# The low part of the forget-sum rows, made by VectorE one step earlier, and the rows' memset moved ahead of it

## The chip, the cores and the metric

The kernel runs on one core of a Trainium2 chip. The metric is the device time in microseconds of one launch. The engines that matter here are TensorE (PE in the profile, its weight loads PEld), VectorE (DVE), ScalarE (ACT) and SyncE (SP), which issues the loads of the weights. Every engine works through its own instructions in order, and they are tied by semaphores.

## The reference, cut to what matters

The program is one DeltaNet block followed by two hybrid layers (L = 0 and 1) on 256 positions of width 1024. The change is in the forgetting attention of the hybrid layers, with 8 heads of 128 channels:

```
log_f = log_sigmoid(ff + b_f)                 # (256 positions, 8 heads)
cum   = cumsum(log_f, axis=positions)
s     = q . k / sqrt(128) + (cum[query] - cum[key])
s     = where(key <= query, s, -inf)
p     = softmax(s);  o = p . v
```

The term `cum[key]` is the same for all queries of a head, so it is a row over the 256 keys. The kernel adds it to the scores by one matmul. That matmul rounds its operands, so each row is held as two parts, a rounded high part and a low part that is the rest; the two are added up by the contraction.

## The kernel before

**The stream.** All large weights come as a stream of chunks of 128 x 2048 values (1 MB each), 93 chunks in each hybrid layer. Chunk n goes through four steps. SyncE loads it into one of four slots of `raw` as soon as the chunk four before it is done. ScalarE's `prep(n)` rounds it to the high weights `w_hi`, in one of two slots, when TensorE is done with chunk n-2. VectorE's `prep(n)` (line 1612) subtracts that from `raw` and so makes the low weights `w_lo`. TensorE then does 48 matmuls in each of two halves, high by high, low by high and high by low (lines 351 to 353, called by `mm3`). ScalarE last copies the result out of PSUM (line 1082 in these stages).

**The order.** It is written out by hand for each engine. In the loop `group(off, after)`, step c of VectorE and ScalarE prepares chunk off+c+2 first, and then runs what the list `after[c]` holds. TensorE does chunk off+c and then its own `after[c]`. So at step c, VectorE's extra work sits behind low weights that can be made only when TensorE has finished chunk off+c, since these need the high weights, and the high weights need the slot of that chunk.

**The forget sums.** VectorE's `ff_log` makes the negated log forget gates and spreads them into `nlf_rep`. TensorE's `cum`, behind its second chunk of the group `L_FV` (c = 1), sums them into PSUM bank 7: columns 16 to 31 for the queries, and columns 256 to 511 of partitions 0 to 63 for the keys' rows. VectorE's `cum` (line 2140) copies the first of these, ScalarE's `row_hi` (line 1439) waits for that copy and then writes the high part of the rows into `fox_rows`, and VectorE's `row_lo` subtracts it from PSUM (line 2149) and copies a last piece (line 2150). The tile `fox_rows` has 128 partitions; those from 64 on are set to zero once, by a memset in `row_lo` of L = 0 (line 2147).

**The scores.** TensorE waits for those rows behind its third chunk (c = 2) and makes the scores of heads 0 to 3; the fourth chunk follows, and then heads 4 to 7:

```
def fox_scores(h0):
    if h0 == 0:
        pe.wait_ge(S("evicted"), j0 + L_FV)
        pe.wait_ge(S("row_ready"), L + 1)
...
        mm(ps[:, bank, 0:P + T], sel_r[:, h:h + 1].to_broadcast([P, P]), fox_rows[:, :], start=True, stop=False, skip_group_check=True)
        mm(ps[:, bank, 0:P], q[:, 0:P], k[:, 0:P], start=False, stop=True, skip_group_check=True)
        mm(ps[:, bank, P:P + T], q[:, P:T], k, start=False, stop=True, skip_group_check=True)\
...
group(tok_chunk, L_FV, 1, [None, cum, lambda: fox_scores(0), lambda: fox_scores(4)])
```

These three matmuls have the lines 933 to 935. VectorE's `fox_scores` takes each head out of PSUM by two instructions (lines 2156 and 2157); for heads 4 to 7 TensorE waits until the head four before has been taken out, as they share a bank. ScalarE's list for the same group is `[None, row_hi]`. In what follows, the chunks of the group `L_FV` are called first, second, third and fourth, and the one behind them is the first of the group `L_RQK`.

Of the kernel before, what the change touches and what calls it, by code (L numbers as in the profile page):

```python
# [16 lines left out]
P = 128  # L17
# [73 lines left out]
def build_program(nc, io, layers=LAYERS):  # L91
    f32, f32r = mybir.dt.float32, mybir.dt.float32r
# [5 lines left out]
    with ctx:  # L98
# [9 lines left out]
        def at(name, shape, offset, dt=f32):  # L108
            return nc.alloc_sbuf_tensor_at(name, shape, dt, offset=offset)
# [21 lines left out]
        fox_rows = at("fox_rows", [P, 3 * P], place[0] + 4 * N_CB, f32r)  # L131
# [29 lines left out]
        def S(name):  # L161
            if name not in sems:
                sems[name] = ctx.enter_context(nc.semaphore(name))
            return sems[name]
# [24 lines left out]
        def bmid(ap, n):  # L189

            ap = ap.unsqueeze(1)
            return ap.to_broadcast([ap.shape[0], n, ap.shape[2]])
# [1410 lines left out]
        def _(dve):  # L1603
            order = Order(dve, "dve_order")
# [3 lines left out]
            def prep(n, s4, s2):  # L1608
                if isinstance(n, int) and n >= total:
                    return  # L1610
                dve.wait_ge(S("hi_ready"), n + 1)
                tt(w_lo[:, s2, :], raw[:, s4, :], w_hi[:, s2, :].bitcast(f32), ALU.subtract).then_inc(S("lo_ready"), 1)  # L1612
# [91 lines left out]
            def softplus(dst, z, e, m, n):  # L1704

                t1, t2 = sm[:, 11, 0:n], z
                order(ts(t1, e, 2.0, None, ALU.add))
                order(nc.vector.reciprocal(t1, t1))
                order(tt(t2, e, t1, ALU.mult))
                order(tt(t1, t2, t2, ALU.mult))  # L1710
                order(ts(e, t1, 1.0 / 17, 1.0 / 15, ALU.mult, ALU.add))
                for odd in (13, 11, 9, 7, 5, 3, 1):
                    order(tt(e, e, t1, ALU.mult))
                    order(ts(e, e, 1.0 / odd, None, ALU.add))
                order(tt(e, e, t2, ALU.mult))
                order(stt(dst, e, 2.0, m, ALU.mult, ALU.add))
# [375 lines left out]
            for L in range(layers):  # L2092
# [17 lines left out]
                def group(off, after=(), n0=n0):  # L2110

                    for c in range(4):
                        n = n0 + off + c
                        prep(n + 2, (n + 2) % RAW, n % 2)
                        for f in (after[c] if c < len(after) else ()):
                            f()
# [12 lines left out]
                def ff_log():  # L2129
                    dve.wait_ge(S("ff_exp"), L + 1)  # L2130
                    softplus(sm[:, 0, 0:16], sm[:, 2, 0:16], sm[:, 3, 0:16], sm[:, 0, 0:16], 16)

                    order(ts(sm[:, 1, 0:16], sm[:, 0, 0:16], math.sqrt(P), None, ALU.mult))
                    for t in range(2):
                        ins = nc.vector.tensor_copy(nlf_rep[:, t, :].rearrange("p (r h) -> p r h", h=8), bmid(sm[:, 1, t * 8:t * 8 + 8], 8))
                    ins.then_inc(S("nlf_ready"), 1)
# [6 lines left out]

                def row_lo():
                    dve.wait_ge(S("row_hi"), L + 1)
                    if L == 0:
                        order.mark(nc.vector.memset(fox_rows[64:P, :].bitcast(f32), 0.0))
                    rows_hi = fox_rows[32:64, P:3 * P]
                    order(tt(rows_hi, ps[32:64, 7, T:2 * T], rows_hi.bitcast(f32), ALU.subtract))
                    nc.vector.tensor_copy(fox_rows[0:64, 0:P], fox_rows[0:64, P:2 * P].bitcast(f32)).then_inc(S("row_ready"), 1)  # L2150

                def fox_scores(h0):
                    for h in range(h0, h0 + 4):
                        bank = 4 + h % 4
                        dve.wait_ge(S("fox_s_mm"), L * 8 + h + 1)
                        order.mark(stt(fox_s[:, h, 0:P], ps[:, bank, 0:P], sm[:, 5, h:h + 1], fm[:, P:T], ALU.add, ALU.add))
                        stt(fox_s[:, h, P:3 * P], ps[:, bank, P:3 * P], sm[:, 5, 8 + h:9 + h], fm, ALU.add, ALU.add)\
                            .then_inc(S("fox_s_ev"), 1)
# [154 lines left out]

                job(n0 + L_FQK, 4)
                group(L_FQK + 4, [[lam], [], [ff], [ff_log]])
                group(L_FV, [[], [cum], [row_lo, lambda: fox_scores(0)], [lambda: fox_scores(4)]])
                group(L_RQK, [[fox_max], [], [], [fox_norm]])
                group(L_RV)
                group(L_LX, [[lo_of(sp_ + 1, s4, 0)], [rope_sin], [rope_cos], [rope_add]])
# [190 lines left out]
```

## Time and profile before

| what | value |
|---|---|
| time, median of 3 runs | 1783.1 us (1782.43 to 1783.38) |
| profiled execution, its own time | 1776.84 us |
| its span, first to last instruction | 1775.0 us |
| TensorE matmuls busy | 1681.6 us, 95% of the span |
| VectorE busy | 1099.2 us, 62% |
| ScalarE busy | 813.8 us, 46% |
| mean granted TensorE clock | 0.988 |
| moved by DMA | 331.40 MB, mean 187 GB/s |

The profiled execution is one execution, and its time lies 1.84 us above its span. Busy times are unions over overlapping instructions. A busy TensorE may still be a slowly clocked one, so the granted clock stands beside it.

### The profile page before, as it was taken

The numbers are of one execution on the slowest core, as the hardware profiler recorded it, in microseconds if no ns is written. First come the engines' busy times: TensorE is split into PE (matmuls) and PEld (weight loads), VectorE is DVE, ScalarE is ACT, GpSimd is POOL, SyncE is SP. The second block draws the span as 40 slices with busy tenths as digits, with TensorE's granted clock in tenths as the row PEclk, the third lists the DMA queues.
The fourth block names the chain that finished last, engine by engine and source line by source line (L and its number), as shares of the span: only waits on it lengthen the run. The fifth ranks groups of instructions, "written<-read, shape, count | busy, mean of one in ns | idle before, by whom it ended". The sixth has DMA issues, their size and how long they took to land.

```text
span 1775.0 us, 34458 instructions
## 1 busy us (share of the span) xinstructions
PE 1681.6 (95%) x15290; PEld 1585.4 (89%) x15290; DVE 1099.2 (62%) x1379; ACT 813.8 (46%) x1053; POOL 34.3 (2%) x68
## 2 busy tenths in 40 slices
PE   5998899999999989999999999989899999999997
PEld 4896788799988889999999899979899999979997
DVE  4476754589853555568775755565547778666463
ACT  3335424433333535447655444435354575445352
POOL 0000000000000000000000000000000000000000
PEclk8999999999999999999999999999999999999999
DMA  9776533564558445545455355535354445535551
GB/s 393 281 286 235 195 145 129 207 214 165 211 211 324 177 155 157 175 146 188 167 190 188 114 190 197 179 107 190 122 188 167 167 167 191 190 111 194 194 190 71
DMA packets 45529, 331.40 MB, mean 187 GB/s; under 512 B 5072, under 2 KB 5072, under 8 KB 5456
## 3 DMA queue, kind: packets, MB, share of 16 engines
q1 hardware_dynamic: 36032, 260.73, 42.7%
q0 software_dynamic: 9216, 67.11, 10.0%
q8 instruction: 113, 1.85, 0.4%
q10 hardware_dynamic: 144, 1.51, 0.2%
q14 instruction: 24, 0.20, 0.0%
HBM read 326.18 MB, written 1.05 MB: 184 GB/s over the span
## 4 chain that ended last, share of the span: by engine, by line
PE 76%; DVE 11%; ACT 7%; DMA 3%; issue 1%; SPq 0%; POOL 0%; ACTq 0%; DVEq 0%; POOLq 0%
PE ps L351 20%; PE ps L352 19%; PE ps L353 19%; DVE w_lo L1612 4%; PE ps L404 4%; ACT w_hi L1071 4%; PE ps L476 3%; PE ps L455 2%; DMA ada_raw<-ada 2%; DMA ada<-ada 1%; PE ps L639 1%; PE ps L650 1%; DVE rstd L1659 1%; DVE rsq L2353 1%; DVE x L1697 1%
## 5 line engine op out<-in xcount | busy, mean ns | idle before, releaser
L1612 DVE TENSOR_TENSOR w_lo<-raw,w_hi 128x2048 fp32r<-128x2048 f32 x207 | 474.4, 2292 | 477.0 <-ACT w_hi L1071 476.6
L351 PE MATMUL ps<-act_hi,w_hi 128*128 128x256 f32 x2672 | 755.2, 283 | 14.2 <-DVE act_lo L1681 4.6
L352 PE MATMUL ps<-act_lo,w_hi 128*128 128x256 f32 x2672 | 743.8, 278 | 0.0
L353 PE MATMUL ps<-act_hi,w_lo 128*128 128x256 f32 x2672 | 743.7, 278 | 0.0
L1071 ACT ACTIVATE w_hi<-raw 128x2048 fp32r<-128x2048 f32 (+1 forms) x229 | 421.9, 1842 | 544.4 <-PE ps L353 527.2
L351 PEld LDWEIGHTS ps<-act_hi,w_hi 128*128 128x128 f32 x2672 | 504.9, 189 | 24.7 <-issue 16.3
L352 PEld LDWEIGHTS ps<-act_lo,w_hi 128*128 128x128 f32 x2672 | 503.5, 188 | 1.1 <-issue 0.2
L353 PEld LDWEIGHTS ps<-act_hi,w_lo 128*128 128x128 f32 x2672 | 503.3, 188 | 0.0
L351 PE MATMUL ps<-mlp_hi,w_hi 128*128 128x256 f32 x512 | 143.3, 280 | 0.4
L352 PE MATMUL ps<-mlp_lo,w_hi 128*128 128x256 f32 x512 | 141.8, 277 | 0.0
L353 PE MATMUL ps<-mlp_hi,w_lo 128*128 128x256 f32 x512 | 141.7, 277 | 0.0
L351 PEld LDWEIGHTS ps<-mlp_hi,w_hi 128*128 128x128 f32 x512 | 96.3, 188 | 1.1 <-DVE w_lo L1620 1.0
L2037 DVE SCALAR_TENSOR_TENSOR gacc<-gpad,vectors,gacc 128x256 f32<-128x256 f32 x176 | 84.5, 481 | 19.7 <-ACT gacc L1344 14.3
L352 PEld LDWEIGHTS ps<-mlp_lo,w_hi 128*128 128x128 f32 x512 | 96.2, 188 | 0.2
L353 PEld LDWEIGHTS ps<-mlp_hi,w_lo 128*128 128x128 f32 x512 | 96.2, 188 | 0.0
L404 PE MATMUL ps<-h_up,raw 128*128 128x256 f32 x352 | 82.4, 386 | 2.0 <-ACT h_up L1334 1.6
L404 PEld LDWEIGHTS ps<-h_up,raw 128*128 128x128 f32 x352 | 65.4, 192 | 13.5 <-ACT h_up L1334 3.0
L351 PE MATMUL ps<-w_hi,act_hi 128*128 128x256 f32 x256 | 72.4, 283 | 0.0
L353 PE MATMUL ps<-w_hi,act_lo 128*128 128x256 f32 x256 | 71.3, 279 | 0.0
L352 PE MATMUL ps<-w_lo,act_hi 128*128 128x256 f32 x256 | 71.3, 278 | 0.0
L476 PE MATMUL ps<-ada_raw,silu_c_wide 128*32 128x256 f32 x1024 | 64.1, 389 | 6.4 <-DMA ada_raw<-ada 6.4
L476 PEld LDWEIGHTS ps<-ada_raw,silu_c_wide 128*32 128x32 f32 x1024 | 30.1, 111 | 30.3 <-DMA ada_raw<-ada 9.0
(414 smaller groups left out, 2015.8 us busy)
## 6 DMA issues: line engine op xcount, KB each, us to landing
raw<-stream SPq DMA_DIRECT2D x233, 1024.0 KB, 4.9
ada_raw<-ada POOLq DMA_DIRECT2D x64, 1024.0 KB, 7.1
ada_f<-ada SPq DMA_DIRECT2D x4, 1024.0 KB, 13.9
ada_a<-ada SPq DMA_DIRECT2D x3, 1024.0 KB, 19.6
s<-s SPq DMA_DIRECT2D x4, 512.0 KB, 10.0
consts_stage<-consts_a SPq DMA_DIRECT2D x1, 1728.0 KB, 32.8
consts_stage<-consts_b ACTq DMA_DIRECT2D x1, 1472.0 KB, 9.8
x<-xT SPq DMA_DIRECT2D x1, 1024.0 KB, 7.0
```

The costliest lines, as they stand in the source:

```text
L351: mm(out, ah, bh, start=first, stop=False, skip_group_check=shared)
L352: mm(out, ah, bl, start=False, stop=False, skip_group_check=shared)
L353: return mm(out, al, bh, start=False, stop=last, skip_group_check=shared)
L404: mm(ps[:, bank, 0:T], raw[:, slot, k * P:(k + 1) * P], h_up[:, k, :], start=k == 0, stop=k == KT - 1)
L455: last = mm(ps[:, 7, 0:T], omean, sq[:, b, :], start=b == 0, stop=b == KT - 1)
L476: last = mm(ps[strip:strip + 32, bank, c * T:(c + 1) * T], cs_wide[:, k, 32 - 3 * j:64 - 3 * j], ada_raw[:, c, k * T:(k + 1) * T], start=j ...
L639: last = mm(ps[r:r + 64, INV_BANK[q], j * 64:(j + 1) * 64], B01[d][r:r + 64, t0 + j // 4, j % 4, r:r + 64], Tm[r:r + 64, q, j, :], start=T ...
L650: last = mm(ps[r:r + 64, INV_BANK[q], j * 32:(j + 1) * 32], Uc[r:r + 64, q, j, :], half(X[r:r + 64, q, j, :], d, 1 << lvl), start=True, st ...
L1071: act_(w_hi[:, s2, o:CH], raw[:, s4, o:CH], ACT.Copy).then_inc(S("hi_ready"), 1)
L1612: tt(w_lo[:, s2, :], raw[:, s4, :], w_hi[:, s2, :].bitcast(f32), ALU.subtract).then_inc(S("lo_ready"), 1)
L1659: nc.vector.reciprocal(rstd[:, :], std[:, :]).then_inc(S("norm_rstd"), 1)
L2037: ins = stt(acc, src, w, acc, ALU.mult, ALU.add)
```

## The change

`row_lo` moves from VectorE's step c = 2 of the group `L_FV` to its step c = 1, right behind `cum`. It was behind the low weights of the chunk that is prepared at c = 2 and is now ahead of them. The memset of `fox_rows`, which only L = 0 has, moves out of `row_lo` into `ff_log`, ahead of the scaling of the log gates. The instructions themselves are the same, and so are those of all other engines.

```diff
@@ -2130,6 +2130,8 @@
                     dve.wait_ge(S("ff_exp"), L + 1)
                     softplus(sm[:, 0, 0:16], sm[:, 2, 0:16], sm[:, 3, 0:16], sm[:, 0, 0:16], 16)
 
+                    if L == 0:
+                        order.mark(nc.vector.memset(fox_rows[64:P, :].bitcast(f32), 0.0))
                     order(ts(sm[:, 1, 0:16], sm[:, 0, 0:16], math.sqrt(P), None, ALU.mult))
@@ -2143,8 +2145,6 @@
 
                 def row_lo():
                     dve.wait_ge(S("row_hi"), L + 1)
-                    if L == 0:
-                        order.mark(nc.vector.memset(fox_rows[64:P, :].bitcast(f32), 0.0))
                     rows_hi = fox_rows[32:64, P:3 * P]
@@ -2313,7 +2313,7 @@
-                group(L_FV, [[], [cum], [row_lo, lambda: fox_scores(0)], [lambda: fox_scores(4)]])
+                group(L_FV, [[], [cum, row_lo], [lambda: fox_scores(0)], [lambda: fox_scores(4)]])
```

## Rows read from the trace of the kernel before

**Rows 1.** The page: granted clock in 40 slices, and the chain by engine.
```profile
PEclk8999999999999999999999999999999999999999
...
PE 76%; DVE 11%; ACT 7%; DMA 3%; issue 1%; SPq 0%; POOL 0%; ACTq 0%; DVEq 0%; POOLq 0%
```

**Rows 2.** TensorE's timeline, L = 0: start, us, line, and idle time before with its releaser.
```profile
655.06 0.28 PE L353 MATMUL ps<-w_hi,act_lo 128*128 128x256 f32 x1
661.49 0.66 PE L933 MATMUL ps<-fox_rows,strip_rows_r 128*128 128x384 f32 x1 [6.15 <-DVE fox_rows L2150]
...
666.08 0.47 PE L351 MATMUL ps<-w_hi,act_hi 128*128 128x256 f32 x1
...
671.80 0.28 PE L353 MATMUL ps<-w_hi,act_lo 128*128 128x256 f32 x1
671.92 0.34 PE L933 MATMUL ps<-fox_rows,strip_rows_r 128*128 128x384 f32 x1
...
675.05 0.47 PE L351 MATMUL ps<-act_hi,w_hi 128*128 128x256 f32 x1
```

**Rows 3.** TensorE's timeline, L = 1.
```profile
1249.95 0.28 PE L353 MATMUL ps<-w_hi,act_lo 128*128 128x256 f32 x1
1255.50 0.66 PE L933 MATMUL ps<-fox_rows,strip_rows_r 128*128 128x384 f32 x1 [5.28 <-DVE fox_rows L2150]
...
1260.05 0.47 PE L351 MATMUL ps<-w_hi,act_hi 128*128 128x256 f32 x1
```

**Rows 4.** The chain in order of time, L = 0: start, us, what.
```profile
655.44 1.92 ACT w_hi L1071
...
657.84 2.29 DVE w_lo L1612
...
660.27 0.38 DVE fox_rows L2147
...
660.67 0.43 DVE fox_rows L2149
...
661.13 0.23 DVE fox_rows L2150
```

**Rows 5.** Busy time by stretch of time; the granted clock stands behind POOL's busy time.
```profile
661.40:664.80 3.40, 3.31 (x12) 3.04 (x13) 0.74 (x2) 0.00 (x0) 0.00 (x0) 0.56 0.02 5
...
670.00:1250.00 580.00, 567.84 (x4692) 550.96 (x4690) 365.02 (x357) 296.15 (x331) 0.00 (x0) 1.00 0.50 169
1260.00:1775.00 515.00, 497.67 (x4142) 485.23 (x4140) 320.21 (x268) 255.45 (x283) 0.00 (x0) 1.00 0.49 164
```

**Rows 6.** ScalarE's timeline, both layers (the high part of the rows).
```profile
652.58 0.38 ACT L1439 ACTIVATE fox_rows<-ps 64x256 fp32r<-64x256 f32 x1 [1.96 <-DVE smalls L2140]
...
1247.47 0.38 ACT L1439 ACTIVATE fox_rows<-ps 64x256 fp32r<-64x256 f32 x1 [1.96 <-DVE smalls L2140]
```

**Rows 7.** VectorE's timeline, L = 0.
```profile
645.75 0.30 DVE L2135 COPY nlf_rep<-smalls 128x64 f32<-128x64 f32 x2
...
645.96 2.29 DVE L1612 TENSOR_TENSOR w_lo<-raw,w_hi 128x2048 fp32r<-128x2048 f32 x1
...
652.38 0.17 DVE L2140 TENSOR_SCALAR smalls<-ps 128x16 f32<-128x16 f32 x1
...
676.34 0.34 DVE L2156 SCALAR_TENSOR_TENSOR fox_s<-ps,smalls,consts_stage 128x128 f32<-128x128 f32 x1
...
678.54 0.48 DVE L2157 SCALAR_TENSOR_TENSOR fox_s<-ps,smalls,consts_stage 128x256 f32<-128x256 f32 x1
```

**Rows 8.** Timeline of TensorE, L = 0: its sums, then the third chunk's first weights.
```profile
647.97 0.28 PE L919 MATMUL ps<-smalls,consts_common 128*128 128x8 f32 x2
...
649.42 0.19 PEld L351 LDWEIGHTS ps<-w_hi,act_hi 128*128 128x128 f32 x1 [0.17 <-issue]
```

**Rows 9.** The tile `raw`: who waited for it (us, times), and its loads' landing times.
```profile
ACT w_hi L1071: 7.3, 3
...
DMA to landing us min/median/max: 4.7/4.9/35.1
```

## The prediction

> **What bounds the kernel now.** I read the page first. TensorE holds 76% of the chain that ended last and its clock is granted in full from the second slice on [rows 1], so the time is TensorE's work plus the places in which it stands still. After 590 us the granted clock is below full only around 660 us and around 1255 us, the place of the change in the two hybrid layers; the two long stretches on either side of the second show 1.00 [rows 5].
>
> So next I took TensorE's timeline there. In L = 0 the last matmul of the third chunk starts at 655.06, and then nothing until the first score matmul at 661.49, with 6.15 us idle that ended on line 2150, the last instruction of `row_lo` [rows 2]. L = 1 has the same with 5.28 us [rows 3].
>
> The chain in order of time says why VectorE is so late: ScalarE's high weights at 655.44 (1.92 us) start only when TensorE is done with the third chunk, VectorE's low weights follow at 657.84 (2.29 us), and behind them in program order the memset (0.38), line 2149 (0.43) and line 2150 (0.23) [rows 4]. The high part that `row_lo` needs was written by ScalarE at 652.58 to 652.96 [rows 6]. The rows wait for a chunk's weights with which they have nothing to do, and those weights aren't wanted by TensorE before the fourth chunk is over.
>
> **`row_lo` moved to step c = 1, the idle.** VectorE's line 2140 starts at 652.38 [rows 7] and ScalarE's answer ends at 652.96 [rows 6]. Lines 2149 and 2150 then take 660.67 to 661.35, that is 0.46 from start to start and about 0.22, and the hand-over to TensorE is 661.49 less 661.35 = 0.14 [rows 2, 4]. With 0.03 for the start, the rows are usable at 652.96 + 0.03 + 0.46 + 0.22 + 0.14 = 653.81. Matmuls follow each other at 0.12, so TensorE gets there at 655.06 + 0.12 = 655.18: 1.37 us of slack. In L = 1 it is 1247.47 + 0.38 + 0.85 = 1248.70 against 1249.95 + 0.12 = 1250.07, again 1.37 [rows 3, 6]. So the wait vanishes altogether. The idle removed is 661.49 - 655.18 = 6.31 in L = 0 and 1255.50 - 1250.07 = 5.43 in L = 1, together 11.74 us [rows 2, 3]. The memset's 0.40 and a late start of the low weights are in the first of these, which is why it is the longer.
>
> **The clock.** After the idle the first 3.4 us of scores ran at a mean of 0.56 of full speed, so mostly at 1.2 GHz and then at 2.4 [rows 5]. Heads 0 to 3 took 666.08 - 661.49 = 4.59 us in L = 0 and 1260.05 - 1255.50 = 4.55 in L = 1. Heads 4 to 7, the same matmuls directly behind a chunk, took 675.05 - 671.92 = 3.13 us [rows 2, 3]. Without the idle heads 0 to 3 come directly behind a chunk too. So 1.46 + 1.42 = 2.88 us come back. The bounds of this term in an execution that isn't profiled: 0, if it wakes at once, and 6.26, if all four heads of both layers ran at half speed (twice 3.13). I take the middle value that both layers show within 0.04. The Trainium skill speaks against taking it so exactly: "TensorE: Matmul & The Clock Gate", section "What's actually happening", says that the number of slow matmuls after an idle differs between runs of one kernel, and that one shouldn't fit to a count. By the page the sum would lie anywhere between these bounds; by the rows it is 2.88. Both layers agree here, which is little evidence against it, and it is a rival below.
>
> **The memset, moved ahead of `nlf_rep` (L = 0 alone).** It is 0.38 us, 0.40 with its gap, in front of line 2133. Bounds: 0 to 0.40. `nlf_rep` is complete at 646.05 and would be at 646.45, while TensorE asks for it at 647.97 [rows 7, 8]. The low weights of the third chunk would end at 645.96 + 2.29 + 0.40 = 648.65, TensorE asks at 649.42, so 0.77 us are left [rows 7, 8]. I take 0. Were that cover gone, it would cost 0.40.
>
> **The new wait.** VectorE now stands for ScalarE's `row_hi`, from about 652.58 to 652.96. Behind it in its queue are the low weights of `L_RQK`'s first chunk. Their high weights aren't there before 655.44 + 1.92 = 657.36 [rows 4], so the 0.4 us are free. No DMA is moved, and SyncE's queue is passed by nothing; its loads follow TensorE's chunks.
>
> **What is late next.** The fourth chunk would start at 655.18 + 3.13 = 658.31, and at the pace of before (666.08 to 671.92, 5.84) end at 664.15 [rows 2]. Its low weights were made at step c = 1. VectorE makes those of `L_RQK` until 660.13 at the latest and then takes out heads 0 to 3, which is 679.02 - 676.34 = 2.68 for four heads [rows 7], so until 662.8. TensorE wants the first of these banks at 664.15: at least 1.3 us of slack. `L_RQK` begins at 664.15 + 3.13 + 0.12 = 667.4, 7 us after its weights. From there on every engine is where it was relative to TensorE. A load has about two chunks' time, over 10 us, until ScalarE wants it, against a median landing of 4.9, and only three of all loads were ever waited for, 7.3 us in total [rows 9]. So the gain should stand to the end.
>
> **Sum.** 11.74 + 2.88 + 0 = 14.62 us, 7.77 in L = 0 and 6.85 in L = 1. The profiled execution goes from 1776.84 to 1762.2, its span from 1775.0 to 1760.4. The median of the runs lies 6.3 us above that execution, a difference that I can't place and carry over unchanged: 1783.1 - 14.6 = 1768.5 us.
>
> **The rivals.**
> - *The clock's part isn't there* (chance 0.05). Either the unprofiled runs resume faster than the profiled one, or the clock falls here even without the idle. For it: the page quoted above, by which that part varies. Against it: 1.46 and 1.42 in two layers, and full clock for heads 4 to 7. Gain 11.74, time 1771.4.
> - *Only one layer gains* (0.03). The rows come late in the other. The point is 1.37 us, by which ScalarE's or VectorE's step would have to slip; each us beyond costs one. At the full loss of one layer the time is 1783.1 - 6.85 = 1776.3 or 1783.1 - 7.77 = 1775.3.
> - *The gain is given back by the weight stream* (0.02). TensorE would have to run into loads that haven't landed, as the whole stream is wanted earlier. Time about 1783. Against it: the 4.9 us to landing.
> - *Slower through the new wait* (0.02). VectorE stands for `row_hi`, and with it the scores and the next low weights. If ScalarE finished at time T, the scores would begin at T + 0.85; this is later than 661.49 from T = 660.64 on, 7.7 us later than the row shows, and costs 1 us per us and layer from there. For 0.2% it takes 9.5 us in both layers: about 1787. Against it: ScalarE was idle for 1.96 us before that instruction [rows 6].
>
> **How the numbers follow.** The sum has 0.88 and gives the predicted 1768.5. Its own range is 1767 to 1770, for the spread of the runs and the hand-over. The clock term's bounds are 14.62 - 2.88 = 11.74 and 11.74 + 6.26 = 18.0, so 1771.4 to 1765.1; I go to 1771.9 on the one side, with the runs' spread of 0.5, and to 1766 on the other, as the deep end needs both layers slow to the last head. That takes in the first rival. A difference under 0.2%, 3.6 us, can't be told from none. Faster: 0.88 + 0.05 + 0.03 = 0.96; same 0.02; slower 0.02.
>
> **What the changed profile would show.** Lines 2149 and 2150 at about 653, right behind line 2140, and the memset near 645.5. No idle time of TensorE ahead of line 933. Heads 0 to 3 in 3.13 us in both layers, and the granted clock 1.00 throughout. VectorE's wait for `row_hi` under 0.5 us. The fourth chunk starting 7.8 us earlier in L = 0, and in L = 1 14.6 us earlier. What would make the forecast wrong: an idle ahead of line 933 that stays, released by line 2150; waits for `raw` further on; or a fallen clock somewhere behind 670 us where before there was none.

## The result, and the profile after

| | before | changed |
|---|---|---|
| first comparison: median (lowest to highest), 9 executions each | 1782.43 us (1775.31 to 1783.85) | 1770.81 us (1768.46 to 1774.55) |
| ratio with its 95% interval | | 0.9941 [0.9927, 0.9955] |
| the profiled execution's span | 1775.0 us | 1766.7 us |
| mean granted clock in it | 0.988 | 0.987 |

The kernel became faster, by 10.5 us by this ratio, where 14.6 were forecast; the interval is 8.0 to 13.0 us. 0.9941 of the 1783.1 us of before is 1772.6, beyond the 1771.9 at which the range ended. (The changed kernel's own median of 1770.81 lies inside the range, but before's median beside it was 1782.43.) All executions of the two kernels, pooled with those that were run later, say 14.1 us (below). So there are two things to explain: what happened at the place of the change, and why one comparison said 10.5.

At the place of the change first. TensorE's timeline of the changed kernel, L = 0, which answers to [rows 2]:

```profile
660.04 0.28 PE L353 MATMUL ps<-w_hi,act_lo 128*128 128x256 f32 x1
660.16 0.34 PE L933 MATMUL ps<-fox_rows,strip_rows_r 128*128 128x384 f32 x1
...
663.29 0.47 PE L351 MATMUL ps<-w_hi,act_hi 128*128 128x256 f32 x1
```

There is no idle mark on line 933 any more: it follows the chunk at 0.12, and heads 0 to 3 take 663.29 - 660.16 = 3.13 us. L = 1 has 0.11 and 3.13 (1247.60 to 1250.73). From the last matmul of the third chunk to the first of the fourth it was 11.02 and 10.10 us [rows 2, 3] and is now 3.25 and 3.24. That is 7.77 and 6.86 us, the forecast's amounts for the two layers to 0.01, with the first profile of before as the other side.

VectorE's timeline, L = 0, which answers to [rows 7] and to the end of [rows 4]:

```profile
651.05 0.38 DVE L2134 MEMSET fox_rows<- 64x384 f32 x1
...
651.67 0.29 DVE L2137 COPY nlf_rep<-smalls 128x64 f32<-128x64 f32 x2
651.88 2.28 DVE L1612 TENSOR_TENSOR w_lo<-raw,w_hi 128x2048 fp32r<-128x2048 f32 x1
...
657.36 0.17 DVE L2142 TENSOR_SCALAR smalls<-ps 128x16 f32<-128x16 f32 x1
658.07 0.42 DVE L2149 TENSOR_TENSOR fox_rows<-ps,fox_rows 32x256 fp32r<-32x256 f32 x1 [0.54 <-ACT fox_rows L1439]
658.52 0.22 DVE L2150 CAST fox_rows<-fox_rows 64x128 fp32r<-64x128 f32 x1
662.36 2.29 DVE L1612 TENSOR_TENSOR w_lo<-raw,w_hi 128x2048 fp32r<-128x2048 f32 x1 [3.62 <-ACT w_hi L1071]
```

The rows are made ahead of the low weights at 662.36. The new wait is 0.54 us on ScalarE's line 1439, and behind it VectorE has nothing to do for 3.62 us until the high weights come. The rows are ready at 658.52 + 0.22 = 658.74, and TensorE wants them at 660.16.

**Where the rest of the difference went.** I cut each profile's span into five stretches: up to the last matmul of the third chunk in L = 0 (front), from there to the fourth chunk (place 0), on to the same matmul in L = 1 (middle), to the fourth chunk there (place 1), and the tail to the end of the span. In us:

| kernel, its profile | front | place 0 | middle | place 1 | tail | span |
|---|---|---|---|---|---|---|
| before | 655.06 | 11.02 | 583.87 | 10.10 | 514.95 | 1775.0 |
| changed | 660.04 | 3.25 | 584.20 | 3.24 | 515.97 | 1766.7 |
| before again (e1) | 661.32 | 12.08 | 582.68 | 11.21 | 517.51 | 1784.8 |
| changed again (e2) | 660.72 | 3.24 | 581.75 | 3.25 | 516.84 | 1765.8 |
| changed, third (e9) | 657.93 | 3.24 | 582.26 | 3.24 | 514.73 | 1761.4 |
| changed, fourth (e10) | 658.33 | 3.25 | 584.58 | 3.24 | 515.00 | 1764.4 |

Between the first two profiles the places give back 14.6 us, and the front (+4.98), the middle (+0.33) and the tail (+1.02) take 6.3 of them, so that 8.3 us of span are left. The places hardly vary for the changed kernel, but the stretches in which it has the same code as before do, the memset of 0.38 us in the front aside. The front of before's first profile, 655.06, is the shortest of all 14 profiles of this study (655.06 to 665.28; the last is that of e7, whose front has the same instructions as the change). So that profile was a quick execution, 6.3 us below the median of the runs, which is what the prediction couldn't place. The second profile of before spans 1784.8, and 6.26 of the 9.8 us between the two lie in the front. What makes a front quick or slow isn't shown.

### The profile page after: what moved, and what is told of

It is laid out like the page before. It is cut to its first block, busy times and chain, and to the rows that moved or that the text cites. A ratio compares the mean times of both kernels' runs of the same rounds, so it can differ in the third digit from the quotient of the medians.

```text
span 1766.7 us, 34458 instructions
## 1 busy us (share of the span) xinstructions
PE 1685.7 (95%) x15290; PEld 1588.8 (90%) x15290; DVE 1098.5 (62%) x1379; ACT 813.3 (46%) x1053; POOL 34.1 (2%) x68
## 4 chain that ended last, share of the span: by engine, by line
PE 78%; DVE 12%; ACT 7%; DMA 2%; issue 1%; SPq 0%; ACTq 0%; DVEq 0%
PE ps L351 20%; PE ps L353 19%; PE ps L352 19%; DVE w_lo L1612 4%; PE ps L404 4%; ACT w_hi L1071 4%; PE ps L455 3%; PE ps L476 3%; DMA ada_raw<-ada 1%; PE ps L639 1%; DVE rstd L1659 1%; PE ps L650 1%; DVE rsq L2353 1%; DVE x L1697 1%; ACT mlp_hi L1577 1%
## 5 line engine op out<-in xcount | busy, mean ns | idle before, releaser
L351 PE MATMUL ps<-act_hi,w_hi 128*128 128x256 f32 x2672 | 755.8, 283 | 15.5 <-DVE act_lo L1681 4.6
```

Source lines behind the costliest of these rows:

```text
L351: mm(out, ah, bh, start=first, stop=False, skip_group_check=shared)
```

## The experiments

All kernels start from one of the two and differ in what the diff shows. "Before" was timed beside each group.

**e1 and e2: the two kernels again.** No edit.

> The kernel before, word for word, timed against itself. Both theories: ratio 1.000, its interval shows the scatter that doubles as noise in the ratio of the change. Its profile is a second sample of the half-clock stretches. Theory 1 (the change gives 7.8 + 6.9 us at its place, and what is missing from 14.6 is chance, because the clock falls at other places in some executions and not in others): idle before line 933 again 6.2 and 5.3 us, but half-clock stretches elsewhere in other places or numbers than in the first profile. Theory 2 (the change itself makes the clock fall further on): the stretches elsewhere are those of the first profile, none near 970 us.

> The changed kernel, word for word, timed again. Theory 1: at the place of the change everything as in its first profile; the ratio to before nearer to 0.992 than 0.9941 was, say 0.990 to 0.995, and the half-clock stretches outside the place at other times than in its first profile. Theory 2: ratio 0.994 again within 0.001, and a half-clock stretch near 970 us again.

Measured: e1 gave a ratio of 1.0005 [0.9985, 1.0025]. e2 gave 0.9917 [0.9892, 0.9942], median 1769.48 against 1783.11 us. The 28 executions of before that stand beside it go from 1775.48 to 1791.02, a spread of 15 us that the three runs shown at first (0.95 us) didn't let one suspect. TensorE's timeline of e1, L = 0:

```profile
667.75 0.66 PE L933 MATMUL ps<-fox_rows,strip_rows_r 128*128 128x384 f32 x1 [6.15 <-DVE fox_rows L2150]
...
669.13 0.88 PE L933 MATMUL ps<-fox_rows,strip_rows_r 128*128 128x384 f32 x1
...
670.73 0.88 PE L933 MATMUL ps<-fox_rows,strip_rows_r 128*128 128x384 f32 x1
...
672.33 0.77 PE L933 MATMUL ps<-fox_rows,strip_rows_r 128*128 128x384 f32 x1
...
673.40 0.47 PE L351 MATMUL ps<-w_hi,act_hi 128*128 128x256 f32 x1
```

and the granted clock in and behind it (the third number from the right):

```profile
667.80:673.40 5.60, 5.60 (x20) 5.03 (x21) 1.95 (x6) 0.00 (x0) 0.00 (x0) 0.55 0.01 3
673.40:679.20 5.80, 5.80 (x50) 5.78 (x49) 1.01 (x3) 0.00 (x0) 0.00 (x0) 1.00 0.00 0
```

The idle is the same to 0.01 us, 6.15, but now almost all four heads ran at 1.2 GHz and they took 5.65 us instead of 4.59. So the clock term isn't a constant of the kernel: the same idle cost 1.46 us in one execution and 2.52 in another. In each of the two executions the two layers agree (1.46 and 1.42, 2.52 and 2.53); the difference is between executions. Theory 1 expected the falls of the clock elsewhere to move between the two profiles of before. In the front one did: there is one at 346.9 us in the first profile and none near it in e1, which has one at 171.0 instead. Behind the first place they didn't: neither has any outside the places before the last 7 us of its span (the end of this section comes back to this).

**e3 and e4: one layer each.**

```diff
-                group(L_FV, [[], [cum, row_lo], [lambda: fox_scores(0)], [lambda: fox_scores(4)]])
+                early = L == 0                      # e4: L == 1
+                group(L_FV, [[], [cum] + ([row_lo] if early else []), ([] if early else [row_lo]) + [lambda: fox_scores(0)],
+                             [lambda: fox_scores(4)]])
```

> The rows are made early in L = 0 only. Theory 1: 7.8 us less than before, ratio 0.9956, and in its profile no idle before line 933 in L = 0 and 5.3 us of it in L = 1, with a half-clock resumption there. Theory 2: about 5 us less (7.8 less a share of what is lost further on), ratio 0.997.

> The rows are made early in L = 1 only; the memset is early as in the change. Theory 1: 6.9 us less than before, ratio 0.9961. With run e3 the two should add up to the ratio of the whole change. Theory 2: about 5 us less, ratio 0.997, and e3 and e4 add up to 10 to 11 us, not to 14.6.

Measured: e3 0.9956 [0.9935, 0.9976] and e4 0.9961 [0.9940, 0.9983], both as theory 1 had them; together 0.0083, as e2's 0.0083. Such an agreement to the last digit is luck, as each interval is 4 us wide to either side. The intervals alone don't exclude theory 2's 0.997; the profiles place what was won. TensorE's timeline of e3 in L = 1, where it still waits, and of e4 in L = 0, where it does:

```profile
1253.57 0.66 PE L933 MATMUL ps<-fox_rows,strip_rows_r 128*128 128x384 f32 x1 [5.28 <-DVE fox_rows L2150]
...
1259.33 0.47 PE L351 MATMUL ps<-w_hi,act_hi 128*128 128x256 f32 x1
```

```profile
661.66 0.66 PE L933 MATMUL ps<-fox_rows,strip_rows_r 128*128 128x384 f32 x1 [5.28 <-DVE fox_rows L2150]
...
666.99 0.47 PE L351 MATMUL ps<-w_hi,act_hi 128*128 128x256 f32 x1
```

Heads 0 to 3 took 5.76 and 5.33 us here. With 4.59 and 4.55 of the first profile and 5.65 and 5.66 of e1 there are six resumptions; their mean is 5.26, or 2.13 us more than the 3.13 without an idle. For two layers that is 4.3 us, not 2.88. The spans of these two profiles, 1781.0 and 1775.0 us, are long by their tails, 521.6 and 522.2 us against 513.9 to 517.5 in the other twelve; the pace of the matmuls makes the difference (last section). A second thing is in e4: it has the memset early, and its idle in L = 0 is 5.28 us, not 6.15.

**e5 and e11: the wait filled with dummy matmuls.** The kernel before, and TensorE isn't idle while it waits.

```diff
                         pe.wait_ge(S("evicted"), j0 + L_FV)
+                        keep_warm(6, 4)
                         pe.wait_ge(S("row_ready"), L + 1)
```

> The kernel before, with six dummy matmuls of 512 columns (3.60 us for four of them at full clock in the first profile, so 5.4 us) put into TensorE's wait for the rows, in both layers. The scores start no earlier, but TensorE isn't idle. It takes the two parts of the gain apart. Theory 1 (idle and clock are two terms): the 11.4 us of waiting stay, but heads 0 to 3 take 3.1 to 3.3 us in both layers instead of 4.6, so 2.9 us less than the first profile, up to 4.9 where an execution resumes as slowly as in run e1; ratio 0.997 to 0.999. Rival (the slow resumption isn't the clock, but the first use of the rows or of PSUM after a wait): heads 0 to 3 take 4.6 us all the same, ratio 1.000.

> The kernel before with the dummy matmuls in the wait, as run e5, once more. e5 gave a mean clock of 0.989, higher than the changed kernel's 0.987, though both have no fall at the place of the change. Theory 1: that was chance, and beside e9 and e10 the two clocks agree within 0.001; ratio 0.997 to 0.9985. Theory 2: the changed kernel's clock stays lower than this one's by 0.001 to 0.002 (4 to 7 us more at half clock).

Measured: 0.9972 [0.9954, 0.9991] and 0.9972 [0.9954, 0.9990]. The timeline of e5, L = 0 (the edit moves the lines by one):

```profile
661.09 0.28 PE L353 MATMUL ps<-w_hi,act_lo 128*128 128x256 f32 x1
661.20 5.31 PE L466 MATMUL ps<-consts_common 128*128 128x512 f32 x12
667.42 0.44 PE L934 MATMUL ps<-fox_rows,strip_rows_r 128*128 128x384 f32 x1 [0.91 <-DVE fox_rows L2151]
...
670.66 0.47 PE L351 MATMUL ps<-w_hi,act_hi 128*128 128x256 f32 x1
```

The scores start no earlier against the chunk (6.33 us behind its last matmul, before 6.43), but they take 3.24 us, in L = 1 and in both layers of e11 too, and the granted clock in these 3.24 us is 1.00. So the slow resumption is the clock after the idle, not the first use of the rows, and the two terms are separate. In time it is 5.0 us by the ratio; by all 24 executions against all of before, 6.0 plus or minus 1.5, and against those of before that stood beside them alone, 5.5 plus or minus 2.0. That is above the 2.88 of the prediction. The second interval holds the 4.3 of the six resumptions, the first (from 4.5 on) just doesn't; whether there is more than the 4.3 stays open.

**e6 and e7: how much slack the rows have.** The changed kernel with 6 and with 14 small instructions ahead of `row_lo`.

```diff
+                def late():
+                    for _ in range(6):              # e7: 14
+                        order(ts(sm[:, 11, 16:32], sm[:, 1, 0:16], 1.0, None, ALU.mult))
+
-                group(L_FV, [[], [cum, row_lo], [lambda: fox_scores(0)], [lambda: fox_scores(4)]])
+                group(L_FV, [[], [cum, late, row_lo], [lambda: fox_scores(0)], [lambda: fox_scores(4)]])
```

> The changed kernel with six small VectorE instructions (0.21 us each) between line 2142 and the wait of row_lo. Some 0.4 us of them lie beside ScalarE's high part, so the rows are 0.9 us later than in the change. If the slack is the 1.37 us of the prediction: no idle before line 933, span within the scatter of the change. If the slack was really smaller than 0.9 us: an idle in both layers.

> The same with fourteen, so the rows come 2.5 us later than in the change. With a slack of 1.3 to 1.4 us: an idle of 1.1 to 1.2 us before line 933 in both layers, and no more than that lost, as the clock doesn't fall in so short an idle: heads 0 to 3 in 3.1 to 3.4 us. If instead an idle of this length also costs clock: heads 0 to 3 in 4.6 us.

Measured, one execution each: 1770.27 and 1772.22 us. e6 has no idle ahead of line 933 in either layer (3.24 us from chunk to chunk), with line 2149 at 1.45 us behind line 2142 instead of 0.71. e7, VectorE and TensorE, L = 0:

```profile
662.60 0.17 DVE L2142 TENSOR_SCALAR smalls<-ps 128x16 f32<-128x16 f32 x1
662.80 2.90 DVE L2318 TENSOR_SCALAR smalls<-smalls 128x16 f32<-128x16 f32 x14
665.73 0.42 DVE L2149 TENSOR_TENSOR fox_rows<-ps,fox_rows 32x256 fp32r<-32x256 f32 x1
666.18 0.22 DVE L2150 CAST fox_rows<-fox_rows 64x128 fp32r<-64x128 f32 x1
```

```profile
665.28 0.28 PE L353 MATMUL ps<-w_hi,act_lo 128*128 128x256 f32 x1
666.55 0.41 PE L933 MATMUL ps<-fox_rows,strip_rows_r 128*128 128x384 f32 x1 [0.98 <-DVE fox_rows L2150]
...
669.75 0.47 PE L351 MATMUL ps<-w_hi,act_hi 128*128 128x256 f32 x1
```

Line 2149 comes 3.13 us behind line 2142, so 2.42 later than in the change, and TensorE is 1.27 - 0.12 = 1.15 us late. The slack is 2.42 - 1.15 = 1.27 us, forecast as 1.37. And heads 0 to 3 take 3.20 us: an idle of 1 us cost its own length and no clock, one of 5.28 or 6.15 us cost clock in all six cases.

**e8: the memset back in `row_lo`, which stays early.** It is out of `ff_log` again, which the cut doesn't show.

```diff
                 def row_lo():
                     dve.wait_ge(S("row_hi"), L + 1)
+                    if L == 0:
+                        order.mark(nc.vector.memset(fox_rows[64:P, :].bitcast(f32), 0.0))
```

> The changed kernel with the memset back in row_lo of L = 0, now at step c = 1. The rows of L = 0 are ready 0.40 us later than in the change, or not later at all where the memset lies beside ScalarE's high part; 1.37 us of slack cover either. No idle before line 933. The place of the memset is worth 0. The other reading, that it was worth the 0.4 to 0.9 us by which the two layers' gains differ, would show as an idle of that size in L = 0.

Measured, one execution: 1771.48 us, and no idle ahead of line 933. But VectorE's timeline shows more than 0.40:

```profile
659.86 0.17 DVE L2140 TENSOR_SCALAR smalls<-ps 128x16 f32<-128x16 f32 x1
661.03 0.38 DVE L2147 MEMSET fox_rows<- 64x384 f32 x1 [1.00 <-ACT fox_rows L1439]
661.44 0.42 DVE L2149 TENSOR_TENSOR fox_rows<-ps,fox_rows 32x256 fp32r<-32x256 f32 x1
```

ScalarE's line 1439 ended at 660.44 (its row: 660.06, 0.38), and the memset starts 0.59 us behind that, where line 2149 of the change starts 0.13 behind it. So the rows come 0.87 us later than in the change, 0.41 for the memset and 0.46 ahead of it. The same 0.87 is the difference between the 6.15 us of L = 0 and the 5.28 of e4. In the slack it cost nothing.

**e9 and e10: the changed kernel for its spread.** No edit.

> The changed kernel once more, word for word, for its spread. All 57 timed executions of the kernel before so far have a mean of 1783.2 us and a mean granted clock of 0.985; 15 of the changed one have 1770.5 us and 0.987. Theory 1 (14.6 us at the place and nothing else): the mean of all executions of the change ends 13 to 15.5 us below that of before, ratio 0.991 to 0.993, and the clock at 0.988, since some 12 us at half clock per execution are gone and nothing came instead. Theory 2, in the form that is left (without the two falls, the clock falls more often at the later norm stages): ratio 0.993 to 0.995 and clock at 0.987 or less.

> The same kernel and the same expectations as run e9; two labels for twice the executions.

Measured: 0.9918 [0.9886, 0.9950] and 0.9917 [0.9885, 0.9948], medians 1765.94 and 1766.13 beside 1783.16 us. All executions of these kernels that were timed, the first comparison's included (mean, 95% of the mean as 1.96 standard deviations over the root of their number, and the granted clock, which the first nine of before lack):

| kernel | executions | mean us | lowest to highest | clock |
|---|---|---|---|---|
| before | 83 | 1783.0 +- 0.9 | 1772.62 to 1791.92 | 0.9847 |
| changed | 27 | 1768.9 +- 1.5 | 1761.55 to 1775.98 | 0.9877 |
| before, wait filled (e5, e11) | 24 | 1777.0 +- 1.2 | 1770.97 to 1782.59 | 0.9886 |

The change is worth 14.1 plus or minus 1.8 us. Without the first comparison (74 and 18 executions) it is 15.3 plus or minus 2.3; against the executions of before that stood beside them it is 14.0 plus or minus 3.1 for e2 and 15.0 plus or minus 3.4 for e9 and e10. Theory 1 keeps its 13 to 15.5; theory 2's 10 to 11 falls. A clock higher by 0.0030 is 2 x 0.0030 x 1776 = 11 us less at half clock in an execution.

**e12: the clock held at the second norm.**

```diff
                 norm_part(ns + 1, a6, 3)
-                keep_warm(4, 6)
+                keep_warm(6, 6)
                 norm(ns + 2, a6)
```

> The changed kernel with six instead of four dummy matmuls ahead of the second norm of each hybrid layer, where TensorE stands still for 1.69 us and the clock fell in some profiles (near 976, 1175 or 1565 us), each fall making that norm 1.1 us longer. Two of them take 1.8 us. If those falls are a part of the scatter: none near 976 and 1565 us any more, and 0 to 2 us less than the changed kernel, so perhaps not to be told from it by time (ratio to before 0.991 to 0.9925). If the dummies are too long for the idle: up to 0.3 us more.

Measured: 0.9895 [0.9869, 0.9921], median 1763.70 (1761.91 to 1765.20). TensorE at this norm in L = 0, first in the changed kernel, then in e12:

```profile
971.55 3.60 PE L466 MATMUL ps<-consts_common 128*128 128x512 f32 x8
976.84 1.13 PE L455 MATMUL ps<-s,consts_common 128*128 128x256 f32 x4 [1.69 <-ACT s L1112]
978.23 4.43 PE L455 MATMUL ps<-s,consts_common 128*128 128x256 f32 x12 [0.26 <-ACT s L1112]
982.50 3.60 PE L466 MATMUL ps<-consts_common 128*128 128x512 f32 x8
```

```profile
968.80 5.31 PE L466 MATMUL ps<-consts_common 128*128 128x512 f32 x12
974.09 1.13 PE L455 MATMUL ps<-s,consts_common 128*128 128x256 f32 x4
975.48 1.13 PE L455 MATMUL ps<-s,consts_common 128*128 128x256 f32 x4 [0.26 <-ACT s L1112]
976.87 1.99 PE L455 MATMUL ps<-s,consts_common 128*128 128x256 f32 x8 [0.26 <-ACT s L1112]
```

The dummies fill the 1.69 us exactly and the norm behind them isn't stretched. It is the fastest kernel of the study and the steadiest, 3.3 us from lowest to highest. Beside e9 and e10 on the same chip its mean is 1763.5 against 1766.9, 3.4 plus or minus 2.8 us less; with 6 and 12 executions, and 0 to 2 us expected, I take this for a likely small gain whose size isn't measured.

**What is left of theory 2.** The clock at the norms of the hybrid layers, by stretches of 40 to 50 us around 980, 1170 and 1565: it is 1.00 in both profiles of before, and it fell once or twice in each of the seven profiles of the changed kernel and its variants e6, e7 and e8. It fell once in e3, e4 and e5 too, and not in e11 and e12. e5 makes the rows as late as before, so a fall there doesn't need the early rows. The changed kernel's first profile, at place 0 and at that norm:

```profile
660.10:663.30 3.20, 3.20 (x23) 3.02 (x22) 0.94 (x1) 2.40 (x2) 0.00 (x0) 1.00 0.65 184
...
978.20:982.70 4.50, 4.47 (x13) 3.69 (x14) 3.79 (x5) 1.26 (x2) 0.00 (x0) 0.64 0.00 0
```

Each such fall costs the norm about 1.1 us (4.43 us from 978.23 on, against 976.87 + 1.99 - 975.48 = 3.38 in e12). Two profiles of before are too few to call it a rule. If it is one, the change gives 11.74 + 4.3 = 16.0 us at its place and loses one or two of them there. 14.1 plus or minus 1.8 doesn't settle it, as the 4.3 is itself uncertain by 0.9 (1.96 standard errors of six resumptions).

## Why the prediction came out as it did

- **The idle, 11.74 us: right.** Gone in all profiles of the changed kernel, 6.31 and 5.44 us; e3 and e4 give it layer by layer. The reading of the chain, that rows ready in ScalarE's part at 652.96 were kept back by weights that nobody needed yet, is shown by e5 too: with the order of before, the scores start as late whatever TensorE does meanwhile.
- **The clock, 2.88 us: the right mechanism, mis-sized.** The prediction took "the middle value that both layers show within 0.04". Two falls of one execution aren't two independent samples of what a typical execution loses: the six resumptions give 4.3 us for two layers, e5 and e11 6.0 plus or minus 1.5. This error alone would have made the gain larger than forecast, not smaller, so it isn't what put the time outside the range. Idles of 6.15 us cost 1.46 and 2.52 us here, and idles of 5.28 us 1.42, 2.53, 2.63 and 2.20 us. The Trainium skill ("TensorE: Matmul & The Clock Gate", section "What's actually happening") warns not to fit to a specific count of slow matmuls, as the count at the start of one and the same kernel differs between runs. The traces agree, for the matmuls behind an idle in the middle of a kernel. The bounds of 0 and 6.26 held all six.
- **The memset, 0 us: right for the change, wrong for its price and for its cover.** At its new place it takes 0.51 us, not 0.40: the changed kernel has 650.74 to 651.46 from the start of line 1716 to that of line 2135, before had 645.33 to 645.54 for the same two. The low weights behind it end at 654.16, and TensorE starts on them at 654.40:

```profile
654.40 0.19 PEld L351 LDWEIGHTS ps<-w_hi,act_hi 128*128 128x128 f32 x1 [0.17 <-DVE w_lo L1612]
```

  That is 0.24 us left where 0.77 was worked out: 0.11 went to the dearer memset and 0.42 to two chunks that ran at 5.44 instead of 5.65 us. In the other profiles with the memset there, 0.23 to 0.66 us were left. TensorE needed 1.57 us from the last matmul ahead of its sums to this one in all 14 profiles, so it lost nothing. In `row_lo` the memset would cost 0.87 (e4, e8). In [rows 4] the low weights start 0.48 us behind the end of the high ones (655.44 + 1.92 to 657.84); in e4, with no memset queued behind them, it is 0.12 (658.40 to 658.52). That lateness goes with the memset; why isn't shown.
- **The new wait and the slack: right.** 0.54 us of wait, slack 1.27 to 1.28 us where 1.37 was worked out; the missing 0.1 is ScalarE's hand-over to line 2149, 0.13 us instead of 0.03. The rivals of a late row and of a slower kernel fall with it. So does the give-back by the weight stream: ScalarE waits for `raw` 7.3 and 7.8 us in the two profiles of before and 6.1, 1.4, 7.7 and 5.9 us in the four of the change; middle and tail scatter instead.
- **What failed is the step from the sum to a time.** "I go to 1771.9 on the one side, with the runs' spread of 0.5": that spread was that of three runs. Single executions of before differ by up to 19 us (1772.62 to 1791.92, standard deviation 4.3), and the first nine of before had a mean of 1781.4, 1.8 below the mean of the 74 later ones, while the first nine of the change lay 3.1 above the mean of its 18 later ones. Both together turn 15.3 into 10.5. With the scatter of all executions the standard error of a difference of two nines is 4.2 x 1.41 / 3 = 2.0 us, so a range for such a comparison had to reach some 4 us to both sides of the best value; and the 6.3 us between the profiled execution and the median was the sign in hand that executions differ by that much. A second sign was read past: the digit 9 of [rows 1] stands for 90% or more, not for the full clock, and the first profile of before has falls at 145.6, 346.9, 507.4 and 579.0 us under it. That the first comparison came out low by chance is the likely reading, not a shown one: the gap of 4.8 us between it and the later ones is about two standard errors, and what else may have differed isn't on record. And that the pooled 14.1 lies so near to the forecast 14.6 is in part luck, as the clock term was 1.4 us too small.

## What to carry to other kernels

When a wait's last releaser is an instruction that had its inputs long before, look at what stands ahead of it in its own queue: moving two instructions of 0.6 us past 2.3 us of work that nobody needed yet gave 14 us of 1783, more than the 11.7 us of the waits themselves, as these idles of 5.28 and 6.15 us also cost clock. Before a range is written, ask how much the same kernel differs from execution to execution in the stretches that the change doesn't touch: a profile whose own time lies 6 us off the median of the runs has already answered.

## What the runs showed of the hardware that I had not expected

- The clock after one and the same idle: heads 0 to 3 took 4.59, 4.55, 5.65, 5.66, 5.76 and 5.33 us behind an idle of 5.28 or 6.15 us, and 3.12 to 3.14 us behind none. An idle of 1.69 us ahead of a sparse stretch was at times enough for a fall to 1.2 GHz, and at times not.
- At a granted clock of 1.00, the same matmuls came at two paces. ScalarE's high weights start when a chunk is done, so their starts give the chunks' length. In the first of these lines, of the changed kernel, it is 5.44 us (647.77 to 653.21) for 48 matmuls (16 each on lines 351 to 353; 48 is the count of a whole chunk, not of each half), and in the kernel before the same chunk took 5.65 (642.57 to 648.22):

```profile
647.77 1.92 ACT L1071 ACTIVATE w_hi<-raw 128x2048 fp32r<-128x2048 f32 x1 [3.04 <-PE ps L353]
...
653.21 1.91 ACT L1071 ACTIVATE w_hi<-raw 128x2048 fp32r<-128x2048 f32 x1 [3.04 <-PE ps L353]
```

```profile
642.57 1.92 ACT L1071 ACTIVATE w_hi<-raw 128x2048 fp32r<-128x2048 f32 x1 [3.26 <-PE ps L353]
...
648.22 1.91 ACT L1071 ACTIVATE w_hi<-raw 128x2048 fp32r<-128x2048 f32 x1 [3.25 <-PE ps L353]
```

  That is 0.113 against 0.118 us per matmul, 4%. It changes from stretch to stretch and from execution to execution. Over the 14 profiles the middle holds 928 (e11) to 2217 (e3) chunk matmuls that start 0.116 to 0.121 us behind the one before, and the tail 809 (e9) to 2678 (e4). A straight line in this count and in the time at half clock, fitted to the 14 profiles, gives 3.9 ns for each such matmul in either stretch. It leaves 0.16 of the 1.7 us by which the middle scatters (580.4 to 586.0 us) and 0.20 of the tail's 2.4 (513.9 to 522.2; standard deviations). So pace and clock make up the scatter there. In the front they don't: 1.2 of 2.7 us are left. What sets the pace I don't know.
- A memset on VectorE delayed what stood next to it: its own start came 0.46 us late in e8, and that of the low weights ahead of it 0.36 late in [rows 4], though it takes 0.38 itself. At its new place in the changed kernel its start is only 0.10 late (651.05, where the instructions ahead of it follow each other at 0.21).
